# Softmax of a latent-attention block: the exponential by its chunk's own maximum instead of the row's

## What is computed

```python
scores = (einsum('bqhd,bkhd->bhqk', qn_b, k_nope) + einsum('bqhd,bkd->bhqk', qr_b, k_rope)) * scale
mask = key_idx[None, :] <= q_idx[:, None]
scores = jnp.where(mask[None, None], scores, -jnp.inf)
p = jax.nn.softmax(scores, axis=-1).astype(v.dtype)
return jnp.einsum('bhqk,bkhd->bqhd', p, v)
```

## Time and profile before

| | |
|---|---|
| median of 3 runs | 2699.91 us (2698.75 to 2700.75) |
| the profiled execution | 2704.03 us, its span 2702.2 us |
| attention in it | 1341 to 2166 us of the span |
| PE | busy 96% of the span, 12186 matmuls |
| DVE | busy 65%, 2073 instructions |
| ACT | busy 31%, 1683 instructions |
| POOL | busy 24%, 592 instructions |
| mean granted clock of PE | 0.984 of full |

### The profile page before, as it was taken

One profiled execution on the slowest core, in us unless ns is written; L12 is line 12 of the kernel. 1 busy time (PEld: TensorE's weight loads), 2 busy tenths in 40 slices (PEclk: granted clock), 3 DMA queues, 4 the chain that ended last, 5 costly groups with the idle time before them and its releaser, 6 DMA issues. The chain is left out here.

```text
span 2702.2 us, 32620 instructions
## 1 busy us (share of the span) xinstructions
PE 2586.2 (96%) x12186; PEld 2127.4 (79%) x12186; DVE 1755.0 (65%) x2073; ACT 850.5 (31%) x1683; POOL 640.9 (24%) x592
## 2 busy tenths in 40 slices
PE   4989999999999999997899999999999999999998
PEld 4767888888888888786677877877878778888887
DVE  5777967979779789564277667667677622223442
ACT  3432111111111111232255555555555520201221
POOL 3132111111111111232032232232232320323422
PEclk8999999999999999999899999999999999999999
DMA  8053212122112121376923112112112164666542
GB/s 298 8 164 116 78 47 78 47 67 83 53 55 78 47 78 48 124 243 240 278 73 107 62 60 107 62 60 107 61 61 86 55 202 156 205 215 211 190 149 78
DMA packets 200833, 306.74 MB, mean 114 GB/s; under 512 B 18234, under 2 KB 119678, under 8 KB 190621
## 3 DMA queue, kind: packets, MB, share of 16 engines
q1 hardware_dynamic: 194604, 284.89, 32.1%
q0 software_dynamic: 6128, 20.45, 2.4%
HBM read 202.01 MB, written 103.28 MB: 113 GB/s over the span
## 5 line engine op out<-in xcount | busy, mean ns | idle before, releaser
L52 PE MATMUL ps_proj<-h_hi,w_hi 128*128 128x512 f32 x1696 | 670.6, 395 | 9.0 <-DVE h_lo L697 6.8
L54 PE MATMUL ps_proj<-h_hi,w_lo 128*128 128x512 f32 x1696 | 663.1, 391 | 0.0
L53 PE MATMUL ps_proj<-h_lo,w_hi 128*128 128x512 f32 x1696 | 663.0, 391 | 0.0
L812 DVE SCALAR_TENSOR_TENSOR acc<-u,taps_t,acc 128x2048 f32<-128x2048 f32 x240 | 629.0, 2621 | 8.5
L52 PEld LDWEIGHTS ps_proj<-h_hi,w_hi 128*128 128x128 f32 x1696 | 320.7, 189 | 77.9 <-issue 8.0
L53 PEld LDWEIGHTS ps_proj<-h_lo,w_hi 128*128 128x128 f32 x1696 | 320.7, 189 | 67.9 <-issue 2.5
L54 PEld LDWEIGHTS ps_proj<-h_hi,w_lo 128*128 128x128 f32 x1696 | 320.2, 189 | 67.4
L586 POOL TENSOR_TENSOR w_lo<-raw,w_hi 128x1024 fp32r<-128x1024 f32 x53 | 168.4, 3177 | 808.5 <-ACT w_hi L411 808.4
L1719 POOL TENSOR_SCALAR prob<-prob,rinv 128x512 f32<-128x512 f32 (+2 forms) x320 | 199.0, 638 | 352.3 <-DVE rinv L1670 352.1
L1675 DVE TENSOR_TENSOR pt_lo<-ps_t,pt_hi 128x512 fp32r<-128x512 f32 (+1 forms) x320 | 194.1, 609 | 96.8 <-ACT pt_hi L1594 93.1
L1594 ACT ACTIVATE pt_hi<-ps_t 128x512 fp32r<-128x512 f32 (+1 forms) x320 | 169.4, 532 | 237.6 <-PE ps_t L1500 237.6
(11 more groups left out here) (220 smaller groups left out, 4037.8 us busy)
## 6 DMA issues: line engine op xcount, KB each, us to landing
qlat<-qlat_dram SPq DMA_DIRECT2D x32, 1024.0 KB, 5.9
raw<-in_w_in_dram SPq DMA_DIRECT2D x52, 512.0 KB, 6.4
under_h<-in_w_ada_dram SPq DMA_DIRECT2D x8, 1024.0 KB, 11.2
ga_dram<-lat SPq DMA_DIRECT2D x8, 1024.0 KB, 5.0
gb_dram<-lat SPq DMA_DIRECT2D x8, 1024.0 KB, 5.0
agate_dram<-lat SPq DMA_DIRECT2D x8, 1024.0 KB, 5.0
conv_dram<-acc SPq DMA_DIRECT2D x8, 1024.0 KB, 3.9
bgate_dram<-lat SPq DMA_DIRECT2D x8, 1024.0 KB, 5.0
```

The costliest lines, as they stand in the source:

```text
L52: pe.matmul(out, wh, xh, start=first, stop=False)
L53: pe.matmul(out, wh, xl, start=False, stop=False)
L54: return pe.matmul(out, wl, xh, start=False, stop=last)
L812: dve.scalar_tensor_tensor(acc[:], u[:, n:n + S], tap(n), acc[:], ALU.mult, ALU.add).then_inc(conv_tap if n < TAPS - 1 else conv_done, 1)
```

## The change

Each chunk's exponential uses that chunk's own maximum (`nmax[:, n, c]`) as soon as it is there, where it used the row's (`nbias`) when all chunks had been seen. ACT then makes one factor per row and chunk, exp(chunk's maximum minus row's maximum), in `share_of`. DVE multiplies the chunk sums by the factors, adds them, takes the reciprocal and multiplies the factors by it; POOL normalises each chunk by its own factor. Group 0, with one chunk, keeps the old arithmetic.

In the list, E(s) comes right behind S(s) for ACT, ahead of the tiles of s. What DVE and POOL did in E is now an event R, at E's old place.

```diff
-            ev.append(("S", s))
+            ev += [("S", s), ("E", s)]
             if s:
-                ev.append(("E", s - 1))
+                ev.append(("R", s - 1))
...
-        ev.append(("E", len(BLOCKS) - 1))
+        ev.append(("R", len(BLOCKS) - 1))
...
                         elif kind == "E":
                             g, b = BLOCKS[n]
-                            act.wait_ge(max_done, at.block(n + 1))
...
                             for c in range(g + 1):
...
+                                if g:
+                                    act.wait_ge(max_step, at.i * (N_CHUNK - QB) + n_max + c + 1)
+                                else:
+                                    act.wait_ge(max_done, at.block(n + 1))
                                 act.activation(prob[:, x:x + width], ps[:, chunk_no[n, c] % RING, 0:width], ACT.Exp,
-                                               bias=nbias[:, n:n + 1],
+                                               bias=nmax[:, n, c:c + 1] if g else nbias[:, n:n + 1],
                                                accum_out=rsum[:, n, c:c + 1]).then_inc(exp_done, 1)
+                            if g:
+                                act.wait_ge(max_done, at.block(n + 1))
+                                act.activation(share_of[:, n, 0:g + 1], nmax[:, n, 0:g + 1], ACT.Exp, scale=-1.0,
+                                               bias=nbias[:, n:n + 1]).then_inc(share_done, 1)
...
-                        elif kind == "E":
+                        elif kind == "R":
                             g, b = BLOCKS[n]
                             dve.wait_ge(exp_done, at.scores(chunk_no[n, g] + 1))
                             if g:
-                                dve.tensor_reduce(rinv[:, n:n + 1], rsum[:, n, 0:g + 1], AX.X,
-                                                  ALU.add).then_inc(sum_step, 1)
-                                dve.wait_ge(sum_step, at.i * (16 - QB) + (n + 1 - QB))
-                                src = rinv[:, n:n + 1]
+                                done = at.i * (3 * (16 - QB)) + 3 * (n - QB)
+                                sums, shares = rsum[:, n, 0:g + 1], share_of[:, n, 0:g + 1]
+                                dve.wait_ge(share_done, at.i * (16 - QB) + (n + 1 - QB))
+                                dve.tensor_tensor(sums, sums, shares, ALU.mult).then_inc(sum_step, 1)
+                                dve.wait_ge(sum_step, done + 1)
+                                dve.tensor_reduce(rinv[:, n:n + 1], sums, AX.X, ALU.add).then_inc(sum_step, 1)
+                                dve.wait_ge(sum_step, done + 2)
+                                dve.reciprocal(rinv[:, n:n + 1], rinv[:, n:n + 1]).then_inc(sum_step, 1)
+                                dve.wait_ge(sum_step, done + 3)
+                                dve.tensor_scalar(shares, shares, rinv[:, n:n + 1], None, ALU.mult).then_inc(rinv_done, 1)
...
-                        elif kind == "E":
+                        elif kind == "R":
...
-                                pool.tensor_scalar(prob[:, x:x + width], prob[:, x:x + width], rinv[:, n:n + 1], 1.0,
+                                pool.tensor_scalar(prob[:, x:x + width], prob[:, x:x + width], share_of[:, n, c:c + 1], 1.0,
                                                    ALU.mult, ALU.mult).then_inc(normed, 1)
```

More of the change, by code:

```diff
@@ L1267, in attention_phase @@
         rsum = sb("rsum", [P, 16, NC_], F32)
+        share_of = sb("share_of", [P, 16, NC_], F32)
         rinv = sb("rinv", [P, 16], F32)
@@ L1291, in attention_phase @@
         sum_step = sem("sum_step")
+        share_done = sem("share_done")
         rinv_done = sem("rinv_done")
@@ L1577, in run @@
                             g, b = BLOCKS[n]
-                            act.wait_ge(max_done, at.block(n + 1))
+                            n_max = chunk_no[n, 0] - QB
                             if b == 0:
@@ L1663, in run @@
                             if g:
-                                dve.tensor_reduce(rinv[:, n:n + 1], rsum[:, n, 0:g + 1], AX.X,
-                                                  ALU.add).then_inc(sum_step, 1)
-                                dve.wait_ge(sum_step, at.i * (16 - QB) + (n + 1 - QB))
-                                src = rinv[:, n:n + 1]
-                            else:
-                                src = rsum[:, n, 0:1]
-                            dve.reciprocal(rinv[:, n:n + 1], src).then_inc(rinv_done, 1)
+                                done = at.i * (3 * (16 - QB)) + 3 * (n - QB)
[8 more added lines that the diff above has]
+                                dve.tensor_scalar(shares, shares, rinv[:, n:n + 1], None, ALU.mult).then_inc(rinv_done, 1)
+                            else:
+                                dve.reciprocal(share_of[:, n, 0:1], rsum[:, n, 0:1]).then_inc(rinv_done, 1)
                         elif kind == "T":
```

## The result

The changed kernel takes **2744.93 us** (median of four runs, 2739.77 to 2746.86) against 2699.39 for the kernel before in the same comparison: 1.0165 times as long, interval 1.0152 to 1.0177. The forecast was 2729 with a range of 2712 to 2746. Direction and mechanism held; the size was 16 us short. The measured time is in the range by 1 us only: the forecast's own terms ended at 2742, and the rest up to 2746 was put on for what I had not seen.

The account below looks back on a forecast made before the run. PE, busy 96% of the span, was taken as the bound. Seven loop heads at +3.0 us (+21) and the last head (+8) gave +29 us, from the median 2699.9 to 2729 us, range 2712 to 2746.

Parts of the forecast that it names:

- the forecast's own terms: Loop heads 2.4 to 3.8 us longer each, last head 3 to 15 us: 2720 to 2742 us, given 77%.
- PE's waits for the banks: Three waits per head for exponentials that free score banks, at s=5, 6 and 7, all go: -1.1 us per head.
- The third tiles: At s=10, 11, 14 and 15, ACT's late copy of the first tile holds PE: +3.7 us per head.
- The working of s=10: First tile's copy starts behind the exponentials and factor, 0.96 us late; less 0.17 us slack, PE stands 0.8 us.
- DVE's two extra steps: Two more 0.18 us steps in R, mostly hidden under the copy wait, but +0.36 us per head at s=9.
- 0.2 us to spare: At s=9, R(7) was said to have about this much slack, so its longer chain would add nothing.
- The clock: a rival in smaller form: Four new stops in every head, each followed by 6 us at half clock, 3 us each: 2825 us; 5%.
- +21: Seven loop heads at +3.0 us each: banks -1.1, third tiles +3.7, DVE's steps +0.4.
- The last head: OW and OA moved up with the exponentials; waits and clock changes sum to 8.1, taken as +8 us.
- behind OW: Last head, s=9: PE stands nearly 4 us behind OW's split, then a slow clock adds 2 us.
- the end: Last head, after s=15: PE's 3.19 us wait shrinks by 1.0, and the clock fall behind it may go: -3.

Follow-up runs that it names:

- the kernel that beat both: Kernel before with chunk maximum, factor and long chain only for s=4 to 7, exponentials early at s=4, 5, 6, POOL's last split a step later: 2688.58 us.
- the kernel with the arithmetic alone: Changed kernel's chunk arithmetic, but tile copies ahead of their block's exponentials and OW and OA placed as in the kernel before: 2713.95 us.

## Why the prediction was right, and where it was short

**PE's waits for the banks: right, slightly low.** They lost 0.28, 0.43, 0.37 and 0.33 us a head, 1.4 and not 1.1, since a fourth was too short to be listed; and the matmul behind each started 0.1 us late as well, which makes 1.8. All went.

**The third tiles: right.** 3.7 us a head was forecast for s=10, 11, 14 and 15; the changed kernel lost 3.8 to 4.1. The working of s=10 gave a copy 0.96 late, measured 1.56 - 0.65 = 0.91. The factor took 0.28 to 0.31 us and was followed after 0.19; I had taken 0.17. The estimate of 0.19 from the figures of the Trainium skill ("ScalarE: Activation LUTs", What ACT_TABLE_LOAD costs) was the better one.

**DVE's two extra steps: the step that failed.** The sum had "Mostly that lies under the wait for the copy", and 0.36 us at s=9. At the third tiles the first part holds. But at s=9 the stop grew by 1.07 us, not 0.36: R(6) took 0.47 longer to POOL (the steps start 0.19 to 0.20 apart, and the last takes 0.23), it started 0.36 later behind ACT's factors at s=5 and 6, which I had left out since no third tile follows there, and R(7), for which I had seen 0.2 us to spare, was held by POOL's split and came 0.23 too late. I had priced the steps by their spacing alone and not looked at what runs beside them and ahead of them. The difference, 0.7 a head, is 5 us in seven.

**The clock: a rival in smaller form.** I dismissed falls of the clock since a 0.89 us wait had left it up. For stops like that one it held: those of 0.7 to 1.2 us at s=11, 14 and 15 left it at 1.00. But at s=9 the stops became about 2 us, and behind these it fell in four heads of seven: 4 x 1.3 = 5 us. The "much longer stops" of my argument needed to be only twice as long. The rival had the mechanism, but at the wrong place and far too often.

These two, 2 us more for the third tiles and 5 less for the banks turn the forecast's +21 into +28, near the loop's +29.4. That the banks' error went the other way is luck.

**The last head: its waits right, its clock wrong.** Forecast and measured, in us lost against before: s=9 +2.9 and +3.3; s=10 +0.8 and +0.7; s=11 +2.9 and +2.8; s=13 +1.5 and +2.2; s=14 +3.1 and +3.1; s=15 0 and -0.1; the end -1.0 and -1.4, with 1.0 more for small waits, one at s=14 and the others behind it. These and the banks (-1.1) give 10.5 of the 13.4. The other 3 are the clock, where the forecast had -1 (+2 behind OW, -3 at the end): it fell behind the stops at s=9, 11 and 14, and not behind OW's alone; over the last head it averages 0.94 instead of 0.96. Moving OW and OA back wins 6.4 us of the 13.4, so about half lay in their place; the other 7.0 I put down to the late copies, the longer chain and the clock, without a run that parts them.

Loop and last head together are +42.8 us; the profiled execution is only 35.7 longer, because the attention starts 7.0 us earlier in it (1353.92 against 1360.96), which the change doesn't touch. That start moves from one execution to the next: in the fourteen profiles of this case it lies between 1353.9 and 1362.4 us. Up to it the granted clock averaged 0.99 in the changed kernel's profile and 0.97 in that of the kernel before. The profiled execution is thus an early one, and the three longer ones, 5 to 7 us above it, had a mean clock of 0.981 to 0.984 over the span instead of 0.988. Whether their heads or what comes ahead of them was slower is not shown. The spread of 7 us isn't owed to the change: ten executions of the kernel before, beside the first experiments, lie between 2695.85 and 2704.75.

## What to carry to other kernels

Work put ahead of a copy on an in-order engine is paid for where the chain behind that copy has only two buffers: write down the slack of the third tile before moving anything, and move only where the bound engine waits for what is moved. A correction that looks small, four steps instead of two on columns of 2 to 4 elements, is a latency, so it costs where the chain is what the next engine waits for: use the new arithmetic only for the blocks that need it, as the kernel that beat both does. And look for what stands behind a stop: here stops of 2 us and more often cost again in clock.

## What the runs showed of the hardware

**A small DVE instruction waits for a running POOL one.** Timelines of DVE and POOL in the last head of the changed kernel:

```profile
2123.18 1.80 DVE L1676 TENSOR_TENSOR rsum<-rsum,share_of 128x2 f32<-128x2 f32 x1
...
2122.63 2.34 POOL L1719 TENSOR_TENSOR o_w_lo<-o_raw,o_w_hi 128x1024 fp32r<-128x1024 f32 x1 [0.51 <-ACT o_w_hi L1561]
2124.95 1.36 POOL L1733 TENSOR_SCALAR prob<-prob,share_of 128x512 f32<-128x512 f32 x2
```

A product of two columns, 0.16 us elsewhere, took 1.80 and ended at 2124.98, with POOL's split at 2124.97. At s=9 the `TENSOR_SCALAR` of four columns ends at 1487.59 and POOL's split at 1487.57; this comes in all eight heads, at 0.82 or 0.83 us each. The reciprocal and the reduction that ran in between, with one input each, took their usual 0.16. POOL's normalisation holds such a step too: the product of s=8 took 0.52 us in seven of the eight heads and ended with one of its chunks. A low part of 512 columns, with one of its two inputs in PSUM, kept its 0.68 to 0.69 us in all 82 cases where POOL was normalising when it started. The products have two inputs in SBUF; the `TENSOR_SCALAR` has one and a value per row, and these runs don't show whether that value counts as a second. The kernel before has a case too, on DVE beside a split of POOL from 1464.02 to 1465.31:

```profile
1464.11 1.74 DVE L1640 TENSOR_TENSOR qr<-rope_a,qr 64x512 fp32r<-64x512 f32 x1
```

0.69 is usual there. The Trainium skill ("SBUF — State Buffer", Who interferes with whom) says that a DVE instruction with two SBUF inputs and a GpSimd one that reads SBUF exclude each other, and that the one that comes second waits for the whole of the first. The rows agree, and show it for a product of two columns, which can so take as long as what is left of POOL's longest instruction.

**The clock can fall behind a stop of 2 us, and needn't.** With stops of about the same length at s=9 in all seven loop heads (2.04 to 2.08 us lost), it fell in four. Stops of 1.73 us there, in the kernel with the arithmetic alone, left it at 1.00 in all seven.
